# Stick-breaking attention on one core: VectorE forms the argument of the weights first in its step, then takes the next scores and the softplus

## What is computed

```
mask = key_pos[None, :] < q_pos[:, None]
log_keep = jnp.where(mask, jax.nn.log_sigmoid(-z), 0.0)
after = lax.cumsum(log_keep, axis=3, reverse=True) - log_keep
w = jnp.where(mask, jnp.exp(jax.nn.log_sigmoid(z) + after), 0.0)
return jnp.einsum('bhqk,bhke->bhqe', w, vf)
```

## Time and profile before

| | |
|---|---|
| median of 3 runs | 2177.13 us (2176.56 to 2178.64) |
| the profiled execution's own time | 2178.5 us |
| its span, first to last instruction | 2176.4 us |
| mean granted TensorE clock, share of full | 0.975 |
| instructions | 23,882 |
| stick-breaking steps in the trace | 525 to 728 us |

### The profile page before, as it was taken

One profiled execution on the slowest core, in us unless ns is written; L12 is line 12 of the kernel. 1 busy time (PEld: TensorE's weight loads), 2 busy tenths in 40 slices (PEclk: granted clock), 3 DMA queues, 4 the chain that ended last, 5 costly groups with the idle time before them and its releaser, 6 DMA issues. The chain is left out here.

```text
span 2176.4 us, 23882 instructions
## 1 busy us (share of the span) xinstructions
PE 2040.8 (94%) x9584; PEld 1625.4 (75%) x9584; DVE 975.4 (45%) x1133; ACT 669.0 (31%) x939; POOL 541.8 (25%) x260
## 2 busy tenths in 40 slices
PE   6999999999988979989996898799999999999999
PEld 4777888887655667755885686688888888888887
DVE  6456655012555467244443377463433343334334
ACT  5311111233565322346551333232111211121111
POOL 0112212221211143025000121302433443334332
PEclk7999999999999989999997899899999999999999
DMA  8354453334111411170114676500111111111112
GB/s 281 96 147 146 150 168 95 95 88 147 54 39 39 163 57 54 68 280 30 52 58 130 210 241 212 206 20 30 49 49 49 49 49 49 49 49 49 49 48 97
DMA packets 200534, 216.99 MB, mean 100 GB/s; under 512 B 8762, under 2 KB 156346, under 8 KB 200426
## 3 DMA queue, kind: packets, MB, share of 16 engines
q1 hardware_dynamic: 200256, 215.40, 30.9%
q10 hardware_dynamic: 170, 0.07, 0.0%
HBM read 162.85 MB, written 52.59 MB: 99 GB/s over the span
## 5 line engine op out<-in xcount | busy, mean ns | idle before, releaser
L661 PE MATMUL dn_ps<-h_hi,dn_hi 128*128 128x512 f32 (+1 forms) x1120 | 460.8, 411 | 20.2 <-PEq L60 8.3
L663 PE MATMUL dn_ps<-h_hi,dn_lo 128*128 128x512 f32 (+1 forms) x1120 | 441.2, 394 | 0.0
L662 PE MATMUL dn_ps<-h_lo,dn_hi 128*128 128x512 f32 (+1 forms) x1120 | 440.4, 393 | 0.0
L139 POOL TENSOR_TENSOR dn_lo<-dn_raw,dn_hi 128x1024 fp32r<-128x1024 f32 (+1 forms) x69 | 165.6, 2401 | 651.3 <-ACT dn_hi L135 547.3
L661 PEld LDWEIGHTS dn_ps<-h_hi,dn_hi 128*128 128x128 f32 (+1 forms) x1120 | 211.5, 189 | 90.9 <-issue 40.8
L663 PEld LDWEIGHTS dn_ps<-h_hi,dn_lo 128*128 128x128 f32 (+1 forms) x1120 | 211.0, 188 | 48.4
L662 PEld LDWEIGHTS dn_ps<-h_lo,dn_hi 128*128 128x128 f32 (+1 forms) x1120 | 211.7, 189 | 46.0 <-issue 4.4
L1200 DVE TENSOR_TENSOR tl_x<-tl_x,tl_bank 128x512 f32<-128x512 f32 x256 | 173.2, 686 | 133.1 <-PE tl_bank L663 133.1
L156 ACT ACTIVATE dn_out<-dn_ps 128x512 f32<-128x512 f32 (+1 forms) x138 | 81.8, 593 | 458.6 <-PE dn_ps L663 451.0
L1036 POOL TENSOR_TENSOR tl_w_lo<-tl_raw,tl_w_hi 128x1024 fp32r<-128x1024 f32 x64 | 153.5, 2399 | 231.2 <-ACT tl_w_hi L957 231.2
L661 PE MATMUL tl_bank<-tl_h_hi,tl_w_hi 128*128 128x512 f32 x512 | 199.5, 390 | 0.0
(11 more groups left out here) (285 smaller groups left out, 2945.4 us busy)
## 6 DMA issues: line engine op xcount, KB each, us to landing
dn_raw<-w_in_dram SPq DMA_DIRECT2D x70, 512.0 KB, 4.4
ada<-w_ada_dram SPq DMA_DIRECT2D x24, 1024.0 KB, 7.4
proj<-dn_out SPq DMA_DIRECT2D x72, 256.0 KB, 2.2
logits<-dn_out SPq DMA_DIRECT2D x64, 256.0 KB, 2.2
mg_gate<-logits SPq DMA_DIRECT2D x32, 512.0 KB, 5.0
tl_raw<-w_up_dram SPq DMA_DIRECT2D x32, 512.0 KB, 4.0
tl_raw<-w_down_dram SPq DMA_DIRECT2D x32, 512.0 KB, 3.5
wa_qk<-proj SPq DMA_DIRECT2D x6, 1024.0 KB, 16.3
```

Source lines behind the costliest of these rows:

```text
L139: self.nc.gpsimd.tensor_tensor(self.lo_at(j), self.raw_at(j), self.hi_at(j).bitcast(F32), ALU.subtract).then_inc(self.lo_ready, 1)
L661: nc.tensor.matmul(out, w_hi[:, t, :], x_hi[:, t, :], start=begin, stop=False)
L662: nc.tensor.matmul(out, w_hi[:, t, :], x_lo[:, t, :], start=False, stop=False)
L663: mm = nc.tensor.matmul(out, w_lo[:, t, :], x_hi[:, t, :], start=False, stop=end)
```

## The change

In VectorE's loop over the steps, argument(n-3) moves from the third place to the first, ahead of take_scores(n) and softplus(n-1). Nothing else is altered: the same instructions with the same waits and semaphores, 24 of each.

```
             for n in range(N + 3):
+                if n >= 3:
+                    argument(n - 3)
                 if n < N:
                     take_scores(n)
                 if 1 <= n <= N:
                     softplus(n - 1)
-                if n >= 3:
-                    argument(n - 3)
-                if 1 <= n <= N:
                     low_softplus(n - 1)
                 if n >= LAG + 1 and closes(n - LAG - 1):
                     take(segment(n - LAG - 1))
```

## The result

The changed kernel took 2158.4 us (median of 6 runs, 2155.2 to 2165.3) beside 2178.6 us (2176.6 to 2186.1, 6 runs) of the kernel before. The ratio is 0.9907 with a 95% interval of 0.9884 to 0.9929: 20.2 us less by the medians, 15 to 25 by the interval, against a forecast of 2157.4 in a range of 2153 to 2163.5. A later set on one chip gave 0.9894 (0.9879 to 0.9908). The span of the profiled execution fell from 2176.4 to 2156.6 us, by 19.8, where the sum said 19.7. Single executions scatter by 10 us, so that the two agree to 0.1 us is in part luck.

What follows compares the result with a forecast made beforehand. The prediction took TensorE's line of matmuls as the bound, with waits for VectorE's argument as its gaps. It summed 22.4 - 4.1 + 1.4 = 19.7 us off 2177.1, giving 2157.4 us, in a range of 2153 to 2163.5.

Steps and rivals of the forecast that it cites:

- What bounds: TensorE, busy 94% of the span; in this stage it waits 15 times, 18.1 us listed, for VectorE's argument.
- The term of 22.4 us: TensorE's 15 listed and three unlisted waits for the argument all vanish, 22.4 us (22.0 to 22.8) off.
- Given back: Longer TensorE waits for ScalarE's copy of a projection half, once in three turns: 4.1 us lost again (2.5 to 6).
- The bound of 8.15 us behind take_scores: Step 14: TensorE's first piece of the next turn can't start earlier than this, because of ScalarE's copy.
- The clock: The half clock behind step 22's 3.02 us wait goes with that wait: 1.4 us off, ends 0 and 1.4.
- none near 3 us: Claim that no wait left in the stage should come near 3 us, the longest about 2, at step 20.
- Contention: VectorE's low part slowed beside GpSimd's split, argument and take_scores queued behind: nothing added; otherwise 1.22 us in four bound turns, 4.9.
- nothing added to the sum: Claim that the argument behind a slowed low part ends just in time for the next scores, costing no time.
- Late scores: Rival: argument still running when scores land, delaying ScalarE's copy in four bound turns; costs 4.9 us, 2162.3 us; chance 13%.
- More is won: Rival: copy comes earlier or banks free sooner, nothing given back; 23.8 us off, 2153.3 us; chance 7%.
- Slower: Rival: argument at VectorE's queue head holds take_scores in every turn; 5.5 us slower, 2182.6 us; chance 2%.

Runs made afterwards that it cites:

- E1: Changed kernel with ScalarE's serve (projection copy, weight split) moved to the head of its turn: 2152.1 us, ratio 0.9867 to the kernel before, stage 176.78 us.
- E3: Kernel before with the argument first only in turns where n leaves 2 by 3: 2178.0 us, ratio 0.9986, stage 203.14 us.
- E6: Changed kernel with the argument back in third place in turn 22 alone: 2165.1 us in one run, stage 188.35 us.
- E8: Changed kernel with three small VectorE instructions on a spare buffer ahead of take_scores in each turn: 2172.9 us in one run, stage 195.63 us.
- E7: The argument second, between take_scores and softplus, where the changed kernel has it first: 2172.6 us in one run, stage 193.40 us.
- E2: Kernel before, argument in its old third place, with ScalarE's serve moved to the head of its turn: 2179.7 us, ratio 1.0005, stage 206.34 us.
- E5: Kernel before with the argument first in turn 22 alone: 2176.6 us, stage 200.61 us; a second run 2177.0 us, stage 200.62 us.

## Why the prediction was right

**What bounds.** Right: all 15 waits for the argument went, and the earlier trace rows had shown the whole cause in one step.

**The term of 22.4 us.** The waits' share, as a difference, is 19.8 + 4.6 given back (below) - 1.4 of the clock = 23.0 us, 0.6 more than taken. Single turns fit the reading start to start: turn 14 gave 8.91 - 7.29 = 1.62 for the 1.59 predicted from a listed wait of 1.32, turn 17 0.28 for 0.25 that no list shows.

**Given back.** 4.1 predicted. Measured as copy waits that are new: turn 9 0.28 (predicted 0.1), turn 12 0.49 (0.5), turn 15 0.95 (0.95), turn 21 9.70 - 8.64 = 1.06 (1.05), and the tail 30.44 - 30.21 + 1.59 = 1.8 (1.5). Together 4.6. The bound of 8.15 us behind take_scores was met to the hundredth. In this term the two low figures are steps 8 and 23, and they cancel most of the 0.6 above: that the sum met the stage's gain to 0.1 us is luck, since each of the two terms is half a us off. Both low figures are contention, which the prediction put at nothing (below). E1 shows that the term is what I called it. What I had not seen is that such waits and the argument's cover each other within a turn (E3); it doesn't alter the sum for this change, in which no argument wait is left, but it made two expectations wrong.

**The clock.** 1.4 us predicted; turn 22 gave 4.76 us where the wait's share is 3.3. E6 brings wait and half clock back together. In the changed kernel no stretch of the stage stands below the full clock, though it has copy waits of 2.04 and 2.00 us; in E3 one of 2.04 us did have the half clock behind it. So this term was right, but with less margin than "none near 3 us" claimed.

**Contention.** Step 12's low part took 2.23 us beside GpSimd's 3.44 us split, and the argument behind it ended 0.1 us before take_scores: just in time, as worked out. But "nothing added to the sum" was wrong by half a us, in two other turns:

```profile
567.05 2.41 POOL L139 TENSOR_TENSOR dn_lo<-dn_raw,dn_hi 128x1024 fp32r<-128x1024 f32 x1
...
568.04 2.22 DVE L2201 TENSOR_TENSOR sb_plus_lo<-sb_softplus,sb_plus_hi 128x768 fp32r<-128x768 f32 x1 [1.44 <-ACT sb_plus_hi L2254]
570.19 0.68 DVE L2208 TENSOR_TENSOR sb_weight<-sb_z,sb_ps_c 128x512 f32<-128x512 f32 x1
570.79 0.41 DVE L2186 TENSOR_SCALAR sb_z<-sb_ps_z 128x256 f32<-128x256 f32 x1
...
679.50 0.41 POOL L2280 TENSOR_SCALAR_AFFINE_SELECT sb_weight<-sb_weight 128x256 f32<-128x256 f32 x1 [6.33 <-ACT sb_weight L2259]
...
679.52 1.45 DVE L2195 SCALAR_TENSOR_TENSOR sb_softplus<-sb_z,sb_mag 128x1024 f32<-128x1024 f32 x1
```

At the end of turn 7 a low part is slow beside the split, the argument behind it holds take_scores(8) back to 0.81 us behind the start of its scores and not 0.54, and turn 9 waits 0.28 us more for the copy. In E3, where take_scores(8) is on time, turn 9 takes 7.17 us. In turn 23 the softplus is slow beside GpSimd's cut, the copy's wait ends 8.39 us behind take_scores and not 8.15, and those 0.24 us are most of what the tail lost beyond the prediction. In the 14 traces every softplus and low part of the stage that is more than 0.1 us longer than its width takes alone (121 rows) overlaps a GpSimd row. No run moved GpSimd's work alone.

All 24 argument rows lie at 1.22 us or below, while low parts reach 2.28 and softplus rows 2.02. One argument lies wholly beside a split:

```profile
690.04 2.40 POOL L139 TENSOR_TENSOR dn_lo<-dn_raw,dn_hi 128x1024 fp32r<-128x1024 f32 x1 [10.14 <-ACT dn_hi L135]
...
690.95 1.22 DVE L2208 TENSOR_TENSOR sb_weight<-sb_z,sb_ps_c 128x1024 f32<-128x1024 f32 x1 [2.11 <-PE sb_ps_c L2126]
```

That agrees with the rule of the Trainium skill, "SBUF — State Buffer", section "Who interferes with whom", by which the instruction with a single SBUF input isn't held.

**The rivals.** Late scores: E8 shows their path, the copy in a third of the turns, and their price, which with the clock is higher than my 4.9 us for 1.22. In the change itself take_scores came late in four of 24 turns, by 0.27 to 0.58 us (turns 5, 8, 9 and 21), and only turn 8's cost anything, the 0.28 us above. More is won: E1 is that case, and needs another edit. Slower: neither E7 nor E8 came near it. The rest of the kernel passed the gain on, 19.79 us of stage and 19.8 of span, with the 1.26 and 1.25 us around the stage cancelling.

## What to carry to other kernels

In an engine's hand-written order, an instruction whose inputs are a turn old should stand ahead of those that wait for this turn's, above all if another engine waits for it: here it cost next to nothing and took 20 us out. Then ask which result of the same turn comes last next, and measure it from the event that starts its chain; here it was a copy at the end of ScalarE's turn, worth another 7 us once moved to where that engine idles, and worth nothing (E2) before the first move was made. Two waits within one turn overlap, so the worth of removing one depends on the other.

## What the hardware did that I had not expected

The half clock (0.50, 1.2 GHz) kept its place in what was repeated: two executions of the kernel before had it in turn 22, two of E5 in turn 16, and both kernels have the same 2.94 us wait in turn 16. A stretch at half cost 1.4 to 1.6 us here (turn 22 before; turn 16 of E5, 11.71 - 10.10), as much as a wait, and it stood at or behind waits of TensorE from 2.0 to 3.0 us, but not at all of them. Turns of the same order repeated to within 0.05 us from execution to execution, apart from it.
